# Level order in the recurrent heads, an exponential ahead of tile copies, and the output weights loaded during the merge

## The chip, the cores and the metric

The kernel runs on one core of a Trainium2 chip. The metric is the device time of one execution in microseconds; lower is better. The engines are TensorE (PE in the rows), VectorE (DVE), ScalarE (ACT), GpSimd (POOL) and SyncE (SP), each with an instruction queue of its own that runs in order and waits on semaphores.

## What is computed

The reference is a float32 block in two halves for 512 tokens of width 1024, with 256 context tokens in front of them in every recurrence. Three parts matter here. Two of them are recurrences with a decay for every channel, of this form, forwards and backwards, whose sum is the output:

```python
def step(s, inp):                     # one chunk of one head
    qc, kc, vc, gc = inp
    gcum = jnp.cumsum(gc, axis=2)
    decay = jnp.exp(jnp.where(causal[:, :, None],
                    gcum[:, :, :, None, :] - gcum[:, :, None, :, :], -jnp.inf))
    att = jnp.einsum('bhtd,bhtsd,bhsd->bhts', qc, decay, kc)
    o = einsum(att, vc) + einsum(qc * jnp.exp(gcum), s)
    s = exp(glast) * s + einsum(kc * jnp.exp(glast - gcum), vc)
```

In the first half of the block this is gated linear attention (4 heads, keys of 64, log-decay `log_sigmoid(..)/16`). In the second half it is 8 heads with keys of 128 whose forget gate `f = lb + (1 - lb) * sigmoid(x W)` gives `log f` and the keys `1 - f`. The head's output is normalised, multiplied by `silu` of a gate and collected. The third part is the end of the first half: `merged = gates_a * (ya W_a) + gates_b * (yb W_b)` and `merged @ w_o`, added to `x`.

## The kernel before

The kernel is a row of stages. Each is a block of one queue per engine, and a barrier follows it. A dense float32 product is made of three float32r products of halves (`product3`): ScalarE rounds a weight tile (`high`), VectorE or GpSimd takes the rest (`low`), TensorE multiplies. Eight such steps over the width make a lot (384 or 512 columns) in one of two PSUM banks, from which ScalarE copies it (`evict`). The SyncE queue loads weight tiles into two buffers, one tile when the half of the tile two before is made.

**Levels.** A chunk is 128 tokens. Its decay matrix isn't formed: seven levels, of block sizes 1 to 64, each cover the pairs that the level's middle splits. For a level, GpSimd subtracts cumulative logs (`hg_dec`), ScalarE takes the exponential, VectorE multiplies keys and queries (`mixed`, tile `hg_mix`), TensorE makes the products (`products`), and VectorE keeps the part under the level's mask (`kept`, tile `hg_att`). Level 0 is the diagonal. There are two buffers of each.

**Gated heads** (`gated_heads`, 8 heads). A head has 14 units; the order in each queue is written by hand with the unit's number `at`. TensorE first makes one whole head of projections (64 steps, `fill(64)`), and in the units of head h it makes the 64 steps of head h + 1: two forget tiles (lots 0 to 3), query (lot 4), value (5, 6), gate (7). Levels stand in the odd units, 1 to 13. Value and key transposes and the state updates of the forward direction stand at the start, those of the backward direction from unit 8. After unit 14 come 2 steps, the head's output product (`o_done`), 8 steps, and the sum of squares. ScalarE's gate activations for the next head (`forget`) stand in unit 10 with a table load on each side, the logs (`logs`) in unit 12, between two more loads. VectorE's scans of the next head stand after unit 14, around the last `kept`.

```python
for at in range(1, 2 * LV + 1):
    if at % 2 == 1:
        i = level_of(h, (at + 1) // 2)
        act.wait_ge(diff_ready, i)
        act.activation(dec[:, (i - 1) % DEC], ..., ACT.Exp).then_inc(dec_ready, 1)
```

**Pair attention** (`gla_pairs`, two pairs of heads) has the same scheme with 72 steps a pair, 24 of them ahead. Its levels already stand in units 1 to 7, one a unit, and its exponential of level k stands in unit k, behind the tile copies of the units before it. At the start ScalarE waits for three constants and takes the decay gates (`near`, `logs`) before its first `high`; VectorE takes `scans` before its first `low`.

**Merge and output product.** `merge` has eight steps; each loads 1 MB of gate weights and 0.5 MB of branch weights. `output_product` loads `w_o` (eight pieces of 0.5 MB) in its own stage and waits for all of them before its first matmul.

## Time and profile before

| what | value |
|---|---|
| time, median of 3 runs (lowest, highest) | 4791.02 us (4790.4, 4795.41) |
| time of the profiled execution | 4792.93 us |
| its span, first to last instruction | 4791.1 us |
| busy: TensorE, its weight loads, VectorE, ScalarE, GpSimd | 83%, 68%, 53%, 33%, 18% |
| mean granted TensorE clock, as a share of full | 0.902 |
| 195 to 426 us (pair attention): TensorE busy, clock | 177.67 of 231 us, 0.81 |
| 785 to 1010 us (first merge, output product) | 197.50 of 225 us, 0.93 |
| 1275 to 1843 us (gated heads) | 454.35 of 568 us, 0.89 |
| two gate weight loads of the merge, starts | 889.30 and 907.45 us |
| ScalarE: table load; cast of a weight tile; tile copy of 384, 512 columns; log of 768; exponential of a level | 1.28; 1.05; 0.48, 0.58; 0.84; 1.06 us |
| VectorE: rest of a weight tile; a level's two mixes; one keep; last-column difference; states of one direction; gated row | 1.22; 1.3; 0.73; 0.96; 1.8; 0.74 us |
| the same two mixes while GpSimd takes a difference (1590.73 to 1593.2 us) | 2.5 us |
| TensorE: a level's products at full clock | 1.06 us |

How to read it: the busy share of TensorE counts pipelined matmuls, so a busy engine isn't at its peak; granted clock 1.00 is 2.4 GHz and 0.50 is 1.2 GHz. In rows of waits, an engine and line waited for another engine's line: us in total, times, longest. In rows of the timeline: start, length, engine, line, operation, written and read tiles, count, and in square brackets the idle time before it and who ended it. Times are microseconds from the start of the span.

### The profile page before, as it was taken

What the parts mean: (1) busy time and instruction counts of PE and PEld (TensorE: products, weight loads), DVE (VectorE), ACT (ScalarE), POOL (GpSimd) and SP (SyncE); (2) the same over time, 40 slices, a digit from 0 to 9 for tenths busy, and PEclk for the clock granted to TensorE, in tenths of its full rate; (3) what the DMA queues carried; (4) which work ended last, traced back from release to release, by engine and by line L of the source; (5) the groups of instructions that cost most, each with busy time, mean ns of one, the idle gap of its engine ahead of it and who ended that gap; (6) DMA issues with size and microseconds to landing.
All of it is one profiled execution on the core that took longest, in us unless ns stands there. A gap on an engine that the chain in (4) does not pass through costs nothing. (4 is left out here: it accounts for less than half of the span.)

```text
span 4791.1 us, 52357 instructions
## 1 busy us (share of the span) xinstructions
PE 3962.1 (83%) x19735; PEld 3261.4 (68%) x19735; DVE 2516.8 (53%) x4208; ACT 1578.8 (33%) x2341; POOL 884.8 (18%) x445
## 2 busy tenths in 40 slices
PE   6387997869488885788886995698979999999995
PEld 5376986538377775677774552586767878888884
DVE  0354773110466663677774003699975555455555
ACT  0333332110344442455554002333653223223322
POOL 0021001100033321111111110242214422222221
PEclk9697999976689897999998997799999999999998
DMA  3011101223111101111112211232656533333331
GB/s 139 31 31 40 32 19 51 91 101 136 36 40 40 37 30 33 40 45 44 41 45 88 88 44 44 94 118 88 200 194 212 189 128 115 117 122 127 116 116 66
DMA packets 134894, 403.46 MB, mean 84 GB/s; under 512 B 16304, under 2 KB 55072, under 8 KB 125088
## 3 DMA queue, kind: packets, MB, share of 16 engines
q1 hardware_dynamic: 134688, 400.68, 24.7%
q8 instruction: 133, 2.18, 0.2%
q14 instruction: 73, 0.60, 0.0%
HBM read 348.18 MB, written 52.45 MB: 84 GB/s over the span
## 5 line engine op out<-in xcount | busy, mean ns | idle before, releaser
L2486 POOL TENSOR_TENSOR ex_vl<-ex_v,ex_vh 128x1024 fp32r<-128x1024 f32 x80 | 192.0, 2400 | 683.2 <-ACT ex_vh L2474 683.2
L243 PE MATMUL ps<-ex_xh,ex_ul 128*128 128x512 f32 x640 | 249.8, 390 | 8.1 <-DVE ex_ul L2493 8.1
L243 PE MATMUL ps<-hT_high,ma_wl 128*128 128x384 f32 (+1 forms) x576 | 233.0, 404 | 25.7 <-DVE ma_wl L3405 25.7
L244 PE MATMUL ps<-ex_xl,ex_uh 128*128 128x512 f32 x640 | 249.4, 390 | 0.0
L245 PE MATMUL ps<-ex_xh,ex_uh 128*128 128x512 f32 x640 | 249.4, 390 | 0.0
L2470 ACT ACTIVATE ex_ab<-ps 128x512 f32<-128x512 f32 x80 | 47.8, 598 | 610.4 <-PE ps L245 610.4
L243 PE MATMUL ps<-ex_vh,ex_al 128*128 128x512 f32 x640 | 249.0, 389 | 0.0
L244 PE MATMUL ps<-ex_vl,ex_ah 128*128 128x512 f32 x640 | 249.0, 389 | 0.0
L245 PE MATMUL ps<-ex_vh,ex_ah 128*128 128x512 f32 x640 | 249.0, 389 | 0.0
L2512 DVE TENSOR_TENSOR ex_acc<-ex_acc,ps 128x512 f32<-128x512 f32 x160 | 109.8, 688 | 248.0 <-PE ps L245 248.0
L1721 DVE TENSOR_TENSOR mg_sg<-mg_sg,ps 128x512 f32<-128x512 f32 x32 | 22.0, 687 | 405.2 <-PE ps L1691 404.6
L2507 DVE TENSOR_TENSOR ex_al<-ex_af,ex_ah 128x512 fp32r<-128x512 f32 x80 | 198.0, 2475 | 61.0 <-ACT ex_ah L2476 61.0
L150 PE MATMUL ps<-cond,mod_w 128*128 128x2 f32 x768 | 164.1, 352 | 70.3 <-DMA mod_w<-in_w_ada_cols 43.5
L2649 POOL TENSOR_TENSOR hg_dec<-hg_cum 128x512 f32<-128x512 f32 x56 | 82.2, 1469 | 730.4 <-DVE hg_cum L2913 577.6
L243 PE MATMUL ps<-hT_high,hg_wl 128*128 128x384 f32 (+1 forms) x512 | 194.2, 379 | 22.1 <-DVE hg_wl L2889 22.1
L150 PEld LDWEIGHTS ps<-cond,mod_w 128*128 128x128 f32 x768 | 164.0, 333 | 71.0 <-issue 71.0
L3101 POOL TENSOR_TENSOR ma_ce<-ma_ce,ma_c 128x512 f32<-128x512 f32 x64 | 94.5, 1477 | 637.2 <-ACT ma_ce L3304 637.2
L245 PE MATMUL ps<-hT_high,ma_wh 128*128 128x384 f32 (+1 forms) x576 | 206.7, 359 | 0.0
L244 PE MATMUL ps<-hT_low,ma_wh 128*128 128x384 f32 (+1 forms) x576 | 206.5, 359 | 0.0
L244 PE MATMUL ps<-hT_low,hg_wh 128*128 128x384 f32 (+1 forms) x512 | 186.8, 365 | 0.0
L245 PE MATMUL ps<-hT_high,hg_wh 128*128 128x384 f32 (+1 forms) x512 | 185.9, 363 | 0.0
L2218 DVE TENSOR_SCALAR sg_two<-iota,chosenT 128x128 f32<-128x128 f32 x512 | 183.9, 418 | 0.0
(509 smaller groups left out, 10735.0 us busy)
## 6 DMA issues: line engine op xcount, KB each, us to landing
ex_u<-in_peer_u SPq DMA_DIRECT2D x80, 512.0 KB, 4.3
ex_v<-in_peer_v SPq DMA_DIRECT2D x80, 512.0 KB, 4.2
gates_by_expert<-sg_gbuf SPq DMA_DIRECT2D x8, 4096.0 KB, 14.8
ma_w<-in_w_in_ma SPq DMA_DIRECT2D x48, 512.0 KB, 3.6
ev_v<-in_peer_v SPq DMA_DIRECT2D x48, 512.0 KB, 3.6
hg_w<-in_w_in_hg SPq DMA_DIRECT2D x40, 512.0 KB, 3.6
ex_g<-gates_by_expert SPq DMA_DIRECT2D x20, 1024.0 KB, 4.8
mg_wg<-in_w_merge SPq DMA_DIRECT2D x16, 1024.0 KB, 5.0
```

What stands on the lines that cost most here:

```text
L150: mm = pe.matmul(ps[:, n % 2, 2 * a:2 * a + 2], wt[:, a, k, :], conds[:, k, :], start=(k == 0), stop=(k == KD - 1))
L243: pe.matmul(out, a[1], b[0], start=start, stop=False)
L244: pe.matmul(out, a[0], b[1], start=False, stop=False)
L245: return pe.matmul(out, a[0], b[0], start=False, stop=stop)
L1721: link(dve.tensor_tensor(sg[:, n % 2, a, :], sg[:, n % 2, a, :], ps[:, b + 2 + a, :], ALU.mult))
L2218: ins = dve.tensor_scalar(two[:, t0 + a, :], iota, chosenT[:, 1, t:t + 1], chosenT[:, 2, t:t + 1], ALU.is_equal, ALU.mult)
L2470: act.activation(ab[:, j % 2, :], ps[:, j % 2, :], ACT.Gelu).then_inc(h_read, 1)
L2486: pool.tensor_tensor(vl[:, j], v[:, j % 2], vh[:, j].bitcast(F32), ALU.subtract).then_inc(vl_ready, 1)
L2507: dve.tensor_tensor(al[:, j], af[:, j % 2], ah[:, j].bitcast(F32), ALU.subtract).then_inc(al_ready, 1)
L2512: dve.tensor_tensor(acc[:, n // 2, n % 2, :], acc[:, n // 2, n % 2, :], ps[:, 2 + n % VB, :], ALU.add).then_inc(v_read, 1)
L2649: pool.tensor_tensor(ke, crossed(cums[:, h % 2], size, False, True), crossed(cums[:, h % 2], size, False, False), ALU.subtract)
L3101: pool.tensor_tensor(ce[:, i % 2], ce[:, i % 2], cT[:, P * c:P * c + P].unsqueeze(1).to_broadcast([P, J, P]), ALU.mult).then_inc(ce_scaled, 1)
```

## The change

Five edits, all in order or place; none changes what is computed.

1. `gated_heads`: levels stand in units 1 to 7, one a unit; ScalarE takes the exponentials of levels 1 and 2 in unit 1 and of level k + 1 in unit k, in front of that unit's tile copies. Transposes, updates, states, output product (now unit 10), gate activations (unit 8 and 9), logs (unit 10, behind the copy of lot 5), scans (unit 11), weighting and weight halves get new units. The sum of squares of head h stands in unit 2 of head h + 1. The query's activation is taken out of `forget` into `asked`; one table load a head goes. The 64 steps are spread by `FILL`.
2. `gla_pairs`: ScalarE's exponentials likewise one unit ahead.
3. `gla_pairs`: the first two `high` and `low` stand in front of the constants, gates and scans.
4. `merge` may load another tensor's rows during its steps 2 to 7; the first merge loads `w_o`.
5. `output_product` takes loaded weights and then neither loads nor waits.

```diff
         act.preload_act_table_set("natural_log_exp_and_others")
+        high(0)
+        high(1)
         act.wait_ge(const_in, 48)
         near(0, 0, 0)
         near(0, 1, 2)
         logs(0)
-        high(0)
-        high(1)
...
         for h in range(H):
             last, n = h + 1 == H, 6 * h
             for at in range(1, 2 * LV + 1):
-                if at <= LV:
-                    i = level_of(h, at)
+                for lv in (1, 2) if at == 1 else (at + 1,) if at < LV else ():
+                    i = level_of(h, lv)
...
+        low(0)
+        low(1)
+        dve.wait_ge(const_in, 48)
         near(0, 0, 0)
         near(0, 1, 2)
         dve.wait_ge(mask_in, 32)
-        dve.wait_ge(const_in, 48)
         scans(0)
-        for n in range(3):
-            low(n)
+        low(2)
         weighted(0, 0)
...
                 sp.dma_start(bT[:, 2 * g:2 * g + 2, :], b_dram[g]).then_inc(b_in, 16)
+            if n >= 2 and after is not None:
+                for j in range(n - 2, KD if n == KD - 1 else n - 1):
+                    sp.dma_start(after[0][:, j, :], after[1][P * j:P * j + P, :]).then_inc(after_in, 16)
+        if after is not None:
+            sp.wait_ge(after_in, 16 * KD)
 
     @block.gpsimd
     def _(pool):
...
+    loads = w is None
+    w = ctx.enter_context(core.sbuf("op_w", [P, KD, D], F32)) if loads else w
     y = ctx.enter_context(core.sbuf("op_y", [P, 2, 512], F32))
     with core.stage("w_in", "pe_done", "out_done", "dsteps") as (block, w_in, pe_done, out_done, dsteps):
         @block.sync
         def _(sp):
-            for j in range(KD):
-                sp.dma_start(w[:, j, :], w_dram[P * j:P * j + P, :]).then_inc(w_in, 16)
-            sp.wait_ge(w_in, 16 * KD)
+            if loads:
+                for j in range(KD):
+                    sp.dma_start(w[:, j, :], w_dram[P * j:P * j + P, :]).then_inc(w_in, 16)
+                sp.wait_ge(w_in, 16 * KD)
 
         @block.tensor
         def _(pe):
-            pe.wait_ge(w_in, 16 * KD)
+            if loads:
+                pe.wait_ge(w_in, 16 * KD)
             for n in range(8):
                 t, h = n // 2, n % 2
                 for j in range(KD):
...
-    tap("mT1", mT[:])
-    output_product(core, k, mT, d["w_o"], rows, 1.0, [xs[:, t, :] for t in range(NXC)])
+    with core.sbuf("op_w", [P, KD, D]) as w_o:
+        merge(core, k, hT, d["w_merge"], 4, 4, yaT, ybT, b_gate[:], mT, after=(w_o, d["w_o"]))
+        tap("mT1", mT[:])
+        output_product(core, k, mT, d["w_o"], rows, 1.0, [xs[:, t, :] for t in range(NXC)], w_o)
     with core.sbuf("final_g", [P, D], F32) as final_g:
...
-    LOW_AT = (1, 3, 6, 10, 13)
+    FILL = (4, 5, 5, 5, 5, 5, 5, 5, 5, 4, 5, 4, 4, 3)
...
+        def squares(h):
+            pe.wait_ge(sq_ready, h + 1)
+            pe.wait_ge(pre_ready, h + 1)
+            pe.matmul(ps[:, 5, :], k.ones[:], scr[:], start=True, stop=True).then_inc(ss_done, 1)
...
         products(0)
         for at in range(1, 2 * LV + 1):
...
+            if at <= LV:
+                products(at)
+            if at == 1:
+                pe.wait_ge(evicted, lot_of(h, V, 1) + 1)
                 for c in range(NC):
...
+                    mm = pe.transpose(turn(c), v[:, P * c:P * c + P], k.ident[:])
...
-            if at % 2 == 1:
-                products((at + 1) // 2)
-            fill(5 if at <= 8 else 4 if at <= 10 else 2 if at % 2 else 1)
...
-        fill(2)
-        pe.wait_ge(att_kept, (h + 1) * (LV + 1))
-        pe.wait_ge(S_ready, 2 * h + 2)
...
-        mm.then_inc(o_done, 1)
-        fill(8)
...
+            if at == 2:
+                key_rows(0)
+            if at == 3:
+                updates(0)
+            if at == 5:
+                key_rows(1)
+            if at == 6:
+                updates(1)
+            if at == 10:
+                pe.wait_ge(att_kept, (h + 1) * (LV + 1))
+                pe.wait_ge(S_ready, 2 * h + 2)
+                for c in range(NXC):
...
+                mm.then_inc(o_done, 1)
+            if at == 2 and h > 0:
+                squares(h - 1)
+            fill(FILL[at - 1])
+    squares(H - 1)
...
+    def asked(h):
         act.wait_ge(evicted, lot_of(h, Q) + 1)
...
     forget(0)
+    asked(0)
     evict(5)
     evict(6)
     high(5)
     logs(0)
     decays(0, 0)
+    decays(0, 1)
     for h in range(H):
         m, n, last = 8 * (h + 1), 5 * (h + 1), h + 1 == H
         for at in range(1, 2 * LV + 1):
-            dr = 0 if at <= LV else 1
-            u = 2 * h + dr
-            if at % 2 == 1:
-                i = level_of(h, (at + 1) // 2)
+            for lv in (1, 2) if at == 1 else (at + 1,) if at < LV else ():
+                i = level_of(h, lv)
                 act.wait_ge(diff_ready, i)
                 act.activation(dec[:, (i - 1) % DEC], dec[:, (i - 1) % DEC], ACT.Exp).then_inc(dec_ready, 1)
             if at == 1:
                 if h > 0:
-                    squares(h - 1)
+                    act.wait_ge(pre_ready, h)
+                evict(lot_of(h, G))
...
+                high(n + FB)
+            if at == 2 and not last:
+                evict(m)
+            if at == 3 and h > 0:
+                rstd(h - 1)
+            if at in (2, 5):
+                u = 2 * h + (0 if at == 2 else 1)
...
-            if at == 5:
-                decays(h, 1)
-            if at == 10:
+            if at == 4 and not last:
+                evict(m + 1)
+                high(n + Q)
+            if at == 5 and not last:
+                evict(m + 2)
+            if at == 7 and not last:
+                evict(m + 3)
+                high(n + V)
+            if at == 8:
                 act.preload_act_table_set("sigmoid_and_others")
                 if not last:
                     forget(h + 1)
+            if at == 9:
+                if not last:
+                    evict(m + 4)
+                    asked(h + 1)
+                    high(n + G)
                 act.wait_ge(evicted, lot_of(h, G) + 1)
                 opened(h)
-                act.preload_act_table_set("natural_log_exp_and_others")
-            if not last and at == 12:
-                logs(h + 1)
-        if not last:
-            evict(m + 5)
-            decays(h + 1, 0)
-            evict(m + 6)
-            high(n + 5 + FF)
-    squares(H - 1)
+            if at == 10:
+                if last:
+                    act.preload_act_table_set("natural_log_exp_and_others")
+                else:
+                    evict(m + 5)
+                    logs(h + 1)
+            if at == 11:
+                squares(h)
+            if at == 12 and not last:
+                decays(h + 1, 0)
+                decays(h + 1, 1)
+                evict(m + 6)
+            if at == 14 and not last:
+                high(n + 5 + FF)
...
     scan(0, 1)
+    low(5)
+    weighted(0, 0)
     for h in range(H):
-        weighted(h, 0)
+        n, last = 5 * (h + 1), h + 1 == H
         for at in range(1, 2 * LV + 1):
-            if at % 2 == 1:
-                mixed(h, (at + 1) // 2)
-            if at in LOW_AT:
-                low(5 * h + 5 + LOW_AT.index(at))
-            if at == 1 and h > 0:
-                pre(h - 1)
-            if at % 2 == 1:
-                kept(h, (at - 1) // 2)
-            if at == 3 and h > 0:
-                tail(h - 1)
+            if at <= LV:
+                mixed(h, at)
+            if at == 2:
+                low(n + FB)
+            if at <= LV + 1:
+                kept(h, at - 1)
+            if at == 3:
+                weighted(h, 1)
             if at == 4:
                 states(h, 0)
-            if at == 6:
-                weighted(h, 1)
-            if at == 11:
+            if at == 5:
+                low(n + Q)
+            if at == 8:
+                low(n + V)
                 states(h, 1)
-            if at == 12 and h + 1 < H:
+            if at == 9 and not last:
                 affine(h + 1, 0)
                 affine(h + 1, 1)
-                query(h + 1)
+            if at == 10:
+                if not last:
+                    query(h + 1)
+                opened(h)
+                low(n + G)
+            if at == 11 and not last:
+                scan(h + 1, 0)
+                scan(h + 1, 1)
             if at == 12:
-                opened(h)
-        if h + 1 < H:
-            scan(h + 1, 0)
-        kept(h, LV)
-        if h + 1 < H:
-            scan(h + 1, 1)
-    pre(H - 1)
+                pre(h)
+            if at == 13 and not last:
+                weighted(h + 1, 0)
+            if at == 14:
+                low(n + 5 + FF)
+            if at == 5 and h > 0:
+                tail(h - 1)
     tail(H - 1)
```

## Rows read from the trace of the kernel before

**Rows 1.** TensorE's waits in the gated heads, 1275 to 1843 us.

```profile
PE ps L2702 <- DVE hg_mix L2934: 82.8, 20, 7.8
...
PE ps L2742 <- DVE oT L2966: 12.7, 8, 2.2
```

**Rows 2.** Windows: busy of each engine with counts, then clock, DMA share, GB/s.

```profile
1512.68:1579.35 66.67, 56.02 (x321) 52.30 (x321) 42.02 (x57) 32.22 (x45) 20.76 (x14) 0.91 0.13 40
1579.00:1585.00 6.00, 5.66 (x27) 5.68 (x28) 5.96 (x7) 1.82 (x4) 0.00 (x0) 0.68 0.30 90
1595.00:1600.00 5.00, 4.84 (x23) 4.34 (x24) 0.70 (x2) 1.03 (x3) 1.47 (x2) 0.66 0.34 108
1637.00:1640.00 3.00, 2.93 (x13) 2.96 (x14) 2.82 (x8) 0.00 (x0) 0.00 (x0) 0.58 0.00 0
```

**Rows 3.** TensorE's timeline, products of a mixed level in the gated heads.

```profile
1329.85 2.08 PE L2702 MATMUL ps<-hg_mix 128*128 128x128 f32 x8 [0.15 <-DVE hg_mix L2934]
...
1568.87 1.75 PE L2702 MATMUL ps<-hg_mix 128*128 128x128 f32 x8 [3.13 <-DVE hg_mix L2934]
...
1579.35 2.04 PE L2702 MATMUL ps<-hg_mix 128*128 128x128 f32 x8 [6.19 <-DVE hg_mix L2934]
...
1800.31 0.94 PE L2702 MATMUL ps<-hg_mix 128*128 128x128 f32 x7
```

**Rows 4.** TensorE's timeline, first products of successive projection steps at full clock.

```profile
1743.43 0.34 PE L243 MATMUL ps<-hT_high,hg_wl 128*128 128x384 f32 x1
...
1743.96 0.34 PE L243 MATMUL ps<-hT_high,hg_wl 128*128 128x384 f32 x1
...
1791.77 0.40 PE L243 MATMUL ps<-hT_high,hg_wl 128*128 128x512 f32 x1
...
1792.47 0.40 PE L243 MATMUL ps<-hT_high,hg_wl 128*128 128x512 f32 x1
```

**Rows 5.** ScalarE's timeline around its gate activations.

```profile
1633.25 1.28 ACT L2871 ACT_TABLE_LOAD   x1
1634.54 1.06 ACT L2829 ACTIVATE hg_dec<-hg_dec 128x1024 f32<-128x1024 f32 x1
```

**Rows 6.** Timeline of the seam between heads 3 and 4.

```profile
1584.14 1.75 DVE L2913 TENSOR_TENSOR_SCAN hg_cum<-hg_restart,hg_f 128x768 f32<-128x768 f32 x1
...
1585.97 1.86 POOL L2649 TENSOR_TENSOR hg_dec<-hg_cum 128x512 f32<-128x512 f32 x1 [25.81 <-DVE hg_cum L2913]
...
1586.81 1.85 DVE L2923 TENSOR_TENSOR hg_kd<-hg_kd,hg_k 128x768 f32<-128x768 f32 x1
...
1588.58 1.58 DVE L2925 TENSOR_TENSOR hg_qe<-hg_qe,hg_q 128x512 f32<-128x512 f32 x1
...
1589.64 1.06 ACT L2829 ACTIVATE hg_dec<-hg_dec 128x1024 f32<-128x1024 f32 x1 [3.46 <-POOL hg_dec L2650]
```

**Rows 7.** TensorE's timeline, level 7 of the last head.

```profile
1828.47 0.76 PE L2702 MATMUL ps<-hg_mix 128*128 128x128 f32 x2 [2.90 <-DVE hg_mix L2934]
```

**Rows 8.** Timeline of pair attention: weight load, first step, one exponential.

```profile
199.02 0.90 SPq L489 DMA_DIRECT2D gla_w<-in_w_in_gla  x2
...
219.86 0.69 PE L243 MATMUL ps<-hT_high,gla_wl 128*128 128x384 f32 x1 [14.08 <-DVE gla_wl L785]
...
252.92 1.06 ACT L715 ACTIVATE ybT<-ybT 128x1024 f32<-128x1024 f32 x1
```

**Rows 9.** The page's DMA issues: KB each, us to landing.

```profile
hg_w<-in_w_in_hg SPq DMA_DIRECT2D x40, 512.0 KB, 3.6
...
mg_wg<-in_w_merge SPq DMA_DIRECT2D x16, 1024.0 KB, 5.0
```

**Rows 10.** TensorE's waits, 195 to 430 us.

```profile
PE ps L561 <- DVE gla_att L843: 14.0, 8, 3.4
```

**Rows 11.** Timeline around the first output product.

```profile
947.39 3.76 SPq L1736 DMA_DIRECT2D op_w<-in_w_o  x8
...
959.96 2.07 PE L1745 MATMUL ps<-op_w,mT 128*128 128x512 f32 x2 [15.93 <-DMA op_w<-in_w_o]
```

More of the change, by code:

```diff
@@ L1635, in _, with merge @@
                 tail(H - 1)
-def merge(core, k, hT, w_dram, nA, nB, aT, bT, gate_bias, mT, b_dram=None):
+def merge(core, k, hT, w_dram, nA, nB, aT, bT, gate_bias, mT, b_dram=None, after=None):
     nc = core.nc
@@ L1651, in merge @@
         sg = ctx.enter_context(core.sbuf("mg_sg", [P, 2, 2, NX], F32))
-        with core.stage("w_in*2", "g_in", "b_in", "high_ready", "low_ready", "gates_done", "pe_done", "sg_ready", "dsteps", "out_done") as (
-                block, w_in, g_in, b_in, high_ready, low_ready, gates_done, pe_done, sg_ready, dsteps, out_done):
+        with core.stage("w_in*2", "g_in", "b_in", "high_ready", "low_ready", "gates_done", "pe_done", "sg_ready", "dsteps", "out_done",
+                        "after_in") as (
+                block, w_in, g_in, b_in, high_ready, low_ready, gates_done, pe_done, sg_ready, dsteps, out_done, after_in):
             @block.sync
@@ L1722, in _, with output_product @@
                     dve.tensor_tensor(mT[:, n, :], sg[:, n % 2, 0, :], sg[:, n % 2, 1, :], ALU.add).then_inc(out_done, 1)
-def output_product(core, k, mT, w_dram, gate_row, alpha, xs):
+def output_product(core, k, mT, w_dram, gate_row, alpha, xs, w=None):
     nc = core.nc
@@ L2683, in _ @@
                     p = h % 2
-                    pe.wait_ge(evicted, lot_of(h, V, 1) + 1)
-                    for c in range(NC):
-                        mm = pe.transpose(turn(c), v[:, P * c:P * c + P], k.ident[:])
-                        if c in (3, NC - 1):
-                            mm.then_inc(vt_done, 1)
                     def products(lv):
@@ L2703, in products, with key_rows @@
                         mm.then_inc(att_done, 1)
+                    def squares(h):
+                        pe.wait_ge(sq_ready, h + 1)
+                        pe.wait_ge(pre_ready, h + 1)
+                        pe.matmul(ps[:, 5, :], k.ones[:], scr[:], start=True, stop=True).then_inc(ss_done, 1)
+                    def key_rows(dr):
+                        pe.wait_ge(kd_ready, 2 * h + dr + 1)
+                        if dr == 0:
+                            pe.wait_ge(vt_copied, 2 * h + 2)
+                        else:
+                            pe.wait_ge(S_ready, 2 * h + 1)
+                        for c in range(NC):
+                            mm = pe.transpose(turn(c), kds[:, dr, P * c:P * c + P], k.ident[:])
+                            if c in (3, NC - 1):
+                                mm.then_inc(kt_done, 1)
@@ L2705, in _, with updates @@
+                    def updates(dr):
+                        u = 2 * h + dr
+                        pe.wait_ge(kt_copied, 2 * u + 2)
+                        if u > 0:
+                            pe.wait_ge(S_ready, u)
+                        for c in ORDER[dr][:-1]:
+                            mm = pe.matmul(U(c), ktok[:, c, :], vt[:, c, :], start=True, stop=True)
+                        mm.then_inc(u_done, 1)
                     products(0)
                     for at in range(1, 2 * LV + 1):
-                        dr = 0 if at <= LV else 1
@@ L2722, in _ @@
-                        if at in (2, LV + 2):
-                            pe.wait_ge(kt_copied, 2 * u + 2)
-                            if u > 0:
-                                pe.wait_ge(S_ready, u)
-                            for c in ORDER[dr][:-1]:
-                                mm = pe.matmul(U(c), ktok[:, c, :], vt[:, c, :], start=True, stop=True)
-                            mm.then_inc(u_done, 1)
-                    fill(2)
-                    pe.wait_ge(att_kept, (h + 1) * (LV + 1))
@@ L2731, in _ @@
-                    pe.wait_ge(S_ready, 2 * h + 2)
-                    for c in range(NXC):
-                        o = ps[:, 5, P * c:P * c + P]
-                        pe.matmul(o, vt[:, C0 + c, :], att[:, c, :], start=True, stop=False)
-                        for dr in range(2):
-                            slot = ORDER[dr][C0:].index(C0 + c)
-                            mm = pe.matmul(o, S[:, dr, slot, :], qe[:, p, dr, P * c:P * c + P], start=False, stop=(dr == 1))
-                    mm.then_inc(o_done, 1)
@@ L2739, in _ @@
-                    fill(8)
-                    pe.wait_ge(sq_ready, h + 1)
-                    pe.wait_ge(pre_ready, h + 1)
-                    pe.matmul(ps[:, 5, :], k.ones[:], scr[:], start=True, stop=True).then_inc(ss_done, 1)
+                                    mm.then_inc(vt_done, 1)
+                        if at == 2:
[4 more added lines that the diff above has]
+                            key_rows(1)
@@ new lines, in _ @@
+                        if at == 6:
[4 more added lines that the diff above has]
+                            for c in range(NXC):
+                                o = ps[:, 5, P * c:P * c + P]
+                                pe.matmul(o, vt[:, C0 + c, :], att[:, c, :], start=True, stop=False)
+                                for dr in range(2):
+                                    slot = ORDER[dr][C0:].index(C0 + c)
+                                    mm = pe.matmul(o, S[:, dr, slot, :], qe[:, p, dr, P * c:P * c + P], start=False, stop=(dr == 1))
+                            mm.then_inc(o_done, 1)
```

35 lines of the change are left out of this document (1 added, 34 removed).

## The prediction

> **What bounds the kernel now.** The page first: TensorE is busy 83% of the span, no other engine over 53%; but its row in slices dips in the touched stages, and the row of the granted clock with it. The stages follow each other with a barrier between, so only time at the critical engine inside the three touched stages counts: pair attention (195 to 426 us), first merge and output product (785 to 1010), gated heads (1275 to 1843). The chain that ended last covers only the last 30 us of the span and says nothing on them. So I read, in this order, TensorE's waits per stage, the timeline around each wait, and the granted clock after it.
>
> In the gated heads TensorE waits 82.8 us for a mixed level, 20 times, and 12.7 us for the gated row (oT) in front of the sum of squares [rows 1]; its first weight tile isn't touched. The pattern repeats: from one late level to the same one in the next head it is 66.67 us, in which TensorE is busy 56.02; the idle 10.6 are waits of 3.13, 6.19 and, left over, some 1.3 [rows 2, 3]. From head 0 to head 7 the mean is (1800.31 - 1329.85)/7 = 67.2 us [rows 3]. After each pause the clock is granted at half (1.2 of 2.4 GHz) for a while: mean 0.68 in the 6 us after the 6.19, 0.66 in 5 us after the row wait, 0.58 in 3 us after the 3.13 [rows 2]. That loses 6 x 0.32 + 5 x 0.34 + 3 x 0.42 = 1.9 + 1.7 + 1.3 = 4.9 us. A head without pauses is 66.7 - 10.6 - 4.9 = **51.1 us**. Cross-check: a projection step of three products takes 0.53 us on 384 columns and 0.70 on 512 [rows 4]; 48 and 16 of them give 36.6 and leave 14.5 for attention.
>
> Why late: ScalarE runs in order and takes a level every second unit. In units 9 to 12 it first does two table loads of 1.28 and four sigmoids, then the exponential, and another load; meanwhile the level waits [rows 5]. GpSimd stands idle 46 of 67 us [rows 2].
>
> **The change, part by part.**
>
> *Gated heads, inside a head.* The seven levels move to units 1 to 7, an exponential one unit ahead and in front of the tile copies. Need against supply: a unit of TensorE is 1.06 for the level's products plus 4 or 5 steps, so 3.5 to 4.8 us with transposes and updates. A level costs GpSimd 20.76/7 = 3.0 us on average and 3.7 beside VectorE [rows 2, 6], ScalarE 1.06, VectorE 1.3 alone or 2.5 beside GpSimd plus 0.73 to keep it. All are under a unit, with two buffers. I walked the three queues through units 1 to 8 with these durations (the table ahead has the single ones): each level is ready 1 to 3 us before TensorE asks, tile copies and weight halves come before their steps, second states at +48 us from the first level for an output product at +53. So the 3.13, the 6.19 and the row wait go (squares now stand two units behind, in the next head). One table load of four a head goes too, in ScalarE's shadow.
>
> *Gated heads, at the seam.* The next head's logs now stand behind the copy of its value tile, which needs projection step 48 (end of unit 10). Call that t = 0. Copy 0.5; load 1.28, two logs to 3.4; first scan 2.7 to 4.5, difference to 5.4, second scan to 7.2; GpSimd's first level 3.7 to 10.9; exponential 11.9. VectorE meanwhile: difference 8.1, gated product 8.9, weighting 1.85 + 1.58 beside GpSimd to 12.2, weight half 1.22 to 13.4, mixed level 1.3 to 2.5, so ready at 14.7 to 15.9 [rows 6]. TensorE: 8 steps of 0.53 and 8 of 0.70 and the diagonal product, 10.9. It waits 3.8 to 5.0; I take **4.3**, plus 1.9 at half clock as after the 6.19. Queued behind the late level: value transposes, 4 steps, level 2; on VectorE the diagonal's copy. Period 51.1 + 4.3 + 1.9 = 57.3, and I add 0.5 for small waits: 57.8. Seven heads: 7 x (67.2 - 57.8) = 66 us.
> The Trainium skill, ScalarE: Activation LUTs, "What ACT_TABLE_LOAD costs", adds about 1.38 us of drain to each switch of set. The rows show none: a load starts at 1633.25, lasts 1.28, and the exponential starts at 1634.54 [rows 5]. By the page the wait would be about 1.4 longer in each of seven heads, 10 us less gain; the row decides.
>
> *Ends of that stage.* At the first head the sixth weight half now stands ahead of the weighting: level 1 about 1.4 us later; bounds 0 to 3. In the last head there are no steps to hide behind; 28.2 us pass from level 1 to level 7 [rows 3, 7]. VectorE's own queue for that stretch is six mixes (7.8 alone, 15 contended), keeps 5.1, weighting 1.6 to 3.4, states 1.8, tail 1: 17 to 26, I take 22; but the second states (1.8) no longer hide. Gain 4, bounds 0 to 9. The stage: 66 - 1.4 + 4 = **69 us**.
>
> *Pair attention, start.* The weight casts waited for the constants, three activations and two logs; the first projection step starts at 219.86 after 14.08 us of waiting, though its weights were asked for at 199.02 [rows 8]. Now cast and low half come first: landing at about 202.6 by the 3.6 us of such loads [rows 9], cast 1.0, half 1.2, ready before TensorE ends the gate-rate products at 205.8. Logs move 0.8 us later. The 24 steps end at about 222, the diagonal at 223.9; the first level then limits: last tile copy 222.8, cast 1.05, two exponentials, mix at about 227 against 241.5. Gain **14**, bounds 11 and 16.
>
> *Pair attention, levels.* The exponential stood behind a tile copy: it starts at 252.92, right behind a copy that waits for TensorE's lot [rows 8]; the mix and two keeps follow, and TensorE waits 1.4, 3.4, 0.5 and 1.6 us a head: 14.0 in all [rows 10]. One unit ahead they are covered by a unit of 4.9 us on TensorE against 3.9 to 4.3 on VectorE. The 3.4 also costs some 1.3 a head at half clock, as after the 3.13 above. Up to 16.6; the waits at the heads' starts stay, since level 1 is where it was. I take **15**, bounds 7 and 17.
>
> *Output weights.* The loads now start when the product's stage opens, 947.39, and TensorE starts at 959.96 [rows 11]. In the merge there are 18 us between 1 MB pieces that land in 5.0 [rows 9], so 0.5 MB more a step is covered; the last pieces land by about 920. The order costs nothing there: SyncE's queue holds only these loads, and an extra 3 x 0.4 us of issue at the end blocks nobody. TensorE can start where SyncE did, at about 947.9: **12**, bounds 11 and 14 (a shorter half-rate start). The second merge is as before.
>
> *Sum.* 69 + 14 + 15 + 12 = 110 us. The profiled execution took 4792.93 (span 4791.1), 1.9 above the median of 4791.02: 4793 - 110 = 4683, as a median **4681**.
>
> **The rivals.**
> A, forecast: the seam keeps 2 to 7 us: 4660 to 4706. 0.61.
> B, the seam is hidden: logs come earlier than my walk, all pauses go. 7 x (67.2 - 51.5) = 110, stage 113, time 4637. For it: GpSimd and VectorE have room on average (21 and 42 us of 67 [rows 2]). Against: the step-48 copy fixes the logs. 0.09.
> C, the seam keeps 8 to 12 us: contention of GpSimd with VectorE's two-input operations (the 1.85 and 3.7 us [rows 6] are of such an overlap) or one more wait in the chain. Period 61 to 66, stage 26, time about 4724. 0.18. The Trainium skill, GPSIMD Engine Reference, in its table of the engine says its SBUF interfaces are shared with VectorE when that has two SBUF inputs. That speaks against packing the levels, and would make C of a full overlap; the sum above holds that overlap at the seam already.
> D, the gated heads' change does nothing: the pauses move whole to the seam (a late level there costs what two cost before). Only the other 41 us stay: 4750. 0.08.
> E, slower: ScalarE waits for step 48, TensorE's steps 45 to 48 wait behind the output product, which waits for states(1) behind VectorE's value half, behind ScalarE's cast. If that ring closes late, every head stalls at units 10 and 1. It takes 41/7 = 5.9 us a head above 67.2, that is a seam of 20 us instead of 4.3, to cross. By the walk states come 5 us early. At 25 us: about 4820. 0.03. The last 0.01 is within 0.2%.
>
> **How the numbers follow.** Predicted 4681. The range takes A, the near side of B and most of C: 4648 to 4730 (A alone 4660 to 4706). A change of 0.2%, about 10 us, is what a measurement can tell; faster 0.95, same 0.02, slower 0.03.
>
> **What the next profile would show.** TensorE's waits on mixed levels in the gated heads fall from 20 to about 7 to 9, one a head at level 1, sum 30 us plus the last head; no wait on the row of the norm; period 57 to 58 us. Pair attention's first projection step at about 206; waits on kept levels near zero but for level 1. Output product at about 12 us behind the last merge step. The prediction is wrong if waits appear at projection steps (a tile copy or half too late), at value transposes, or at level 2 or 3 because VectorE carries the low half and the weighting in front of them.

## The result, and the profile after

The changed kernel takes **4674.86 us** (median of 4 runs, 4669.97 to 4675.12) against 4792.42 us for the kernel before (4 runs, 4790.4 to 4795.41) on the same chip: 0.9752 of it, interval 0.9735 to 0.9769, or 117.6 us less. The forecast was 110 less. The span is 4673.3 us.

The stages run one behind the other, so the time between the first weight loads of successive stages shows where it went (worked out from the starts of the loads of `gla_w`, `gdn_w`, `mg_wg`, `hg_w`, `proj_w` and the first matmul on `op_w`):

| stretch | before | after | difference | forecast |
|---|---|---|---|---|
| pair attention (`gla_w` to `gdn_w`) | 227.8 | 189.1 | -38.7 | -29 (14 + 15) |
| first merge to its output product (`mg_wg` to `op_w`) | 175.0 | 162.6 | -12.4 | -12 |
| gated heads (`hg_w` to `proj_w`) | 573.2 | 503.4 | -69.8 | -69 |
| all the rest | 3815.1 | 3818.2 | +3.1 | 0 |

The rest is in stages that the change leaves alone. In the thirteen traces of this document, one of each kernel and a second of the changed one, this rest takes 3813.0 to 3820.3 us, so its 3.1 are what differs from trace to trace. Where a run leaves pair attention as it is after the change, the stage repeats within 188.8 to 190.1 us, the merge to its product within 162.1 to 162.6, and the gated heads within 503.4 to 505.6.

**Gated heads.** The changed kernel's TensorE waits from 1210 to 1730 us (engine and line, for whom, us in total, times, longest), which answer to [rows 1] (mixed levels, the stage's first weight tile, the second states, the gated row):

```profile
PE ps L2708 <- DVE hg_mix L2963: 49.6, 13, 10.1
PE ps L243 <- DVE hg_wl L2918: 22.5, 1, 22.5
PE ps L2759 <- DVE hg_S L2984: 2.6, 1, 2.6
PE ps L2714 <- DVE oT L2995: 1.6, 1, 1.6
```

The waits on a mixed level fell from 82.8 to 49.6 us and those in front of the sum of squares from 12.7 to 1.6, once instead of 8 times. Where the 13 stand is in TensorE's timeline, the answer to [rows 3]. The rows are level 1 of heads 0, 2 and 7 (those of heads 1 and 3 to 6 wait 5.05 to 5.07 us), and last, level 7 of head 7:

```profile
1281.63 2.07 PE L2708 MATMUL ps<-hg_mix 128*128 128x128 f32 x8 [10.14 <-DVE hg_mix L2963]
...
1397.46 2.01 PE L2708 MATMUL ps<-hg_mix 128*128 128x128 f32 x8 [5.07 <-DVE hg_mix L2963]
...
1686.94 1.42 PE L2708 MATMUL ps<-hg_mix 128*128 128x128 f32 x8 [3.90 <-DVE hg_mix L2963]
...
1708.10 1.13 PE L2708 MATMUL ps<-hg_mix 128*128 128x128 f32 x8 [0.30 <-DVE hg_mix L2963]
```

One wait a head is left, always at level 1: 10.14 us in the first head, 5.05 or 5.07 in the next six, 3.90 in the last. From the second head on this is the wait at the seam, where a new head's levels follow the units of the head before. Levels 2 to 7 wait for nothing until the last head, where five of them wait 5.2 us together. The period, from level 1 of one head to level 1 of the next, is (1686.94 - 1281.63)/7 = 57.9 us, against 67.2 before. The windows of one head and of the 5 us behind its wait (us, busy of PE, PEld, DVE, ACT, POOL, clock, DMA share, GB/s), beside [rows 2]:

```profile
1397.46:1455.73 58.27, 53.20 (x321) 50.29 (x321) 44.64 (x57) 30.86 (x45) 19.04 (x15) 0.97 0.15 46
1397.46:1402.46 5.00, 5.00 (x24) 5.00 (x25) 3.46 (x4) 2.23 (x5) 4.37 (x4) 0.66 0.12 47
```

The same 321 matmuls keep TensorE busy 53.20 instead of 56.02 us, because the mean clock over a head rose from 0.91 to 0.97. The clock is still granted at half behind the wait that is left (0.66 in 5 us), which loses 5 x 0.34 = 1.7 us.

What the wait is made of shows in the timeline of the seam before head 2 in the changed kernel:

```profile
1381.79 0.48 ACT L2784 COPY hg_v<-ps 128x384 f32<-128x384 f32 x1 [4.13 <-PE ps L245]
...
1382.29 1.28 ACT L2804 ACT_TABLE_LOAD   x1
...
1383.58 1.58 ACT L2807 ACTIVATE hg_f<-hg_f 128x768 f32<-128x768 f32 x2
...
1387.13 1.75 DVE L2942 TENSOR_TENSOR_SCAN hg_cum<-hg_restart,hg_f 128x768 f32<-128x768 f32 x1
...
1388.96 1.88 POOL L2660 TENSOR_TENSOR hg_dec<-hg_cum 128x512 f32<-128x512 f32 x1 [30.48 <-DVE hg_cum L2942]
...
1390.45 1.20 DVE L2952 TENSOR_TENSOR hg_kd<-hg_kd,hg_k 128x768 f32<-128x768 f32 x1
...
1391.58 1.57 DVE L2954 TENSOR_TENSOR hg_qe<-hg_qe,hg_q 128x512 f32<-128x512 f32 x1
1392.56 1.49 POOL L2660 TENSOR_TENSOR hg_dec<-hg_cum 128x512 f32<-128x512 f32 x1
1392.63 1.06 ACT L2856 ACTIVATE hg_dec<-hg_dec 128x1024 f32<-128x1024 f32 x1 [0.57 <-POOL hg_dec L2661]
1393.07 2.06 DVE L2918 TENSOR_TENSOR hg_wl<-hg_w,hg_wh 128x1024 fp32r<-128x1024 f32 x1
...
1395.05 1.66 DVE L2962 TENSOR_TENSOR hg_mix<-hg_dec,hg_k 128x512 f32<-128x512 f32 x1
...
1396.63 0.68 DVE L2963 TENSOR_TENSOR hg_mix<-hg_dec,hg_q 128x512 f32<-128x512 f32 x1
```

ScalarE idles 4.13 us for projection step 48, copies its tile, and only then loads the table and takes the logs. From that copy to the mixed level it is 1397.46 - 1381.79 = 15.7 us; TensorE has other work for 10.6 of them. GpSimd had been idle 30.48 us when its first level could start.

**Pair attention.** TensorE's timeline in the changed kernel, first projection step and level 1 of both pairs:

```profile
205.64 0.69 PE L243 MATMUL ps<-hT_high,gla_wl 128*128 128x384 f32 x1
...
227.07 3.09 PE L561 MATMUL ps<-gla_mix 64*128 64x128 f32 x16 [2.90 <-DVE gla_att L838]
...
310.67 3.09 PE L561 MATMUL ps<-gla_mix 64*128 64x128 f32 x16 [4.38 <-DVE gla_att L838]
```

The first step waits for nothing (14.08 before, [rows 8]). Its waits list has no entry for kept levels under the mask any more (14.0 before, [rows 10]); the two for the diagonal, 7.3 together, stay. From level 1 to level 7 of pair one and of pair two, windows of the kernel before (same columns as above):

```profile
241.50:285.60 44.10, 37.01 (x217) 33.67 (x217) 20.61 (x28) 10.32 (x15) 10.76 (x10) 0.88 0.06 21
334.59:380.51 45.92, 38.88 (x216) 35.61 (x217) 20.62 (x28) 10.31 (x15) 10.17 (x10) 0.83 0.00 1
```

and of the changed kernel:

```profile
227.07:261.70 34.63, 34.63 (x216) 31.75 (x216) 22.64 (x29) 10.43 (x15) 10.80 (x10) 0.91 0.08 27
310.67:344.62 33.95, 33.95 (x217) 31.08 (x217) 22.60 (x29) 10.43 (x15) 10.75 (x10) 0.93 0.00 1
```

The two level stretches are 9.5 and 12.0 us shorter. TensorE's idle time gives 7.1 and 7.0 of that; the other 2.4 and 4.9 are the same matmuls, done in less time at a higher clock. Behind the second pair's level 7 the stage ends 43.5 us later (388.1 - 344.6) instead of 46.3 (426.8 - 380.5); there too it is the clock, 0.71 instead of 0.66, with TensorE busy 31.95 instead of 34.76 us.

**Output product.** Its first matmul in the changed kernel, beside [rows 11]:

```profile
908.90 4.08 PE L1755 MATMUL ps<-op_w,mT 128*128 128x512 f32 x5 [3.47 <-PEq L69]
```

It waits 3.47 us for the stage's barrier where it waited 15.93 for its weights.

### The profile page after: what moved, and what is told of

Its sections match the earlier page's. It is cut to its first block and busy times, and to the rows that moved or that the text cites. A ratio compares the mean times of both kernels' runs of the same rounds, so it can differ in the third digit from the quotient of the medians.

```text
span 4673.3 us, 52352 instructions
## 1 busy us (share of the span) xinstructions
PE 3933.1 (84%) x19735; PEld 3238.1 (69%) x19735; DVE 2539.2 (54%) x4208; ACT 1570.4 (34%) x2334; POOL 872.3 (19%) x445
## 5 line engine op out<-in xcount | busy, mean ns | idle before, releaser
L2660 POOL TENSOR_TENSOR hg_dec<-hg_cum 128x512 f32<-128x512 f32 x56 | 69.9, 1248 | 664.5 <-DVE hg_cum L2942 599.1
```

The costliest lines, as they stand in the source:

```text
L2660: pool.tensor_tensor(ke, crossed(cums[:, h % 2], size, False, True), crossed(cums[:, h % 2], size, False, False), ALU.subtract)
```

## Experiments

All start from the changed kernel; diffs are against it. Each time was measured together with runs of the kernel before (4793.4 us for the first four, 4793.04 for the next four, 4792.52 for the last three), and ratios with their intervals are to that. An interval of 0.0016 on either side is about 8 us, wider than most differences here. So the readings go by stage lengths, taken from one trace of each kernel as in the table above.

### The gated heads as before

The whole function is put back, all else stays.

```diff
 def gated_heads(...):
-    FILL = (4, 5, 5, 5, 5, 5, 5, 5, 5, 4, 5, 4, 4, 3)
+    LOW_AT = (1, 3, 6, 10, 13)
...
+                        if at % 2 == 1:
+                            products((at + 1) // 2)
+                        fill(5 if at <= 8 else 4 if at <= 10 else 2 if at % 2 else 1)
```

> The changed kernel with the gated heads of the kernel before. Theory: the gated heads' part is worth 69 us alone (stage starts 118.9 us earlier after it against 50.2 before it), nothing of it comes from other stages: about 4744, and the stage's rows as before (20 waits on mixed levels, 82.8 us). Rival: the parts help each other (clock carried over from one stage to the next), then the cost of undoing differs from 69 by more than 5 us.

4739.27 us, 0.989 (0.9873 to 0.9906). The stage takes 571.8 us, 68.4 more than in the changed kernel. TensorE's waits in it are back:

```profile
PE ps L2713 <- DVE hg_mix L2945: 80.1, 20, 7.8
...
PE ps L2753 <- DVE oT L2977: 11.2, 8, 2.1
```

The whole run costs 64.4 us more, 4 less than the stage: the stages that no edit touches took 3814.0 us in this trace and 3818.2 in the changed kernel's, which is within their spread. So 68 to 70 us belong to this function; help from other stages of a few us is not excluded by whole runs, but no stage length shows any.

### Pair attention's exponentials back in their own units

```diff
-                        for lv in (1, 2) if at == 1 else (at + 1,) if at < LV else ():
-                            i = level_of(h, lv)
+                        if at <= LV:
+                            i = level_of(h, at)
```

> The changed kernel with pair attention's exponentials back in their own units behind the tile copies; its early casts stay. Theory: this edit alone is worth 24 us, 14 of pauses and 10 of half clock that followed them: about 4699. Rival one: the half clock costs only 1.3 us a head as forecast, and the rest of the 38.7 us of that stage belongs to the early casts: about 4691. Rival two: the pauses are absorbed later in the stage: under 4 us.

4695.09 us, 0.9796 (0.978 to 0.9813). The stage takes 213.2 us, 24.1 more. Its TensorE waits from 195 to 415 us:

```profile
PE ps L561 <- DVE gla_att L843: 14.1, 9, 3.4
```

14.1 us of pauses cost 24.1 us. The other 10 are TensorE's own work at a lower clock: levels 1 to 7 of the first pair (226.46 to 270.59 us of this kernel) take 44.13 us and keep it busy 36.98 at a clock of 0.89, for the 216 matmuls that take 34.63 in the changed kernel; the kernel before has 37.01. The time of the run, 4695.09, lies midway between the 4699 of the theory and the 4691 of rival one and can't tell them apart; the stage's 24.1 us can, since the early casts stayed and rival one allows it 17.

### Only the last three exponentials back

Levels 1 to 4 stay ahead, 5 to 7 stand in their own unit, behind its tile copies.

```diff
-                        for lv in (1, 2) if at == 1 else (at + 1,) if at < LV else ():
+                        for lv in {1: (1, 2), 2: (3,), 3: (4,)}.get(at, (at,) if 5 <= at <= LV else ()):
```

> Exponentials of levels 2 to 4 ahead, those of levels 5 to 7 back in their own units. Only the two smaller pauses of a pair (0.5 and 1.6 us) come back, 4.4 us in all. Theory: a pause this short is not followed by much half clock, so 4 to 6 us above the changed kernel (4679 to 4681) and the 3.4 us pause is what brings the half clock. Rival: half clock follows every pause in proportion: 24 x 4.4/14 = 7.5 us, about 4682 or more.

4680.81 us, 0.9767 (0.9751 to 0.9783). The stage takes 198.3 us, 9.2 more. Three pauses a pair came back, not two. TensorE's waits in it:

```profile
PE ps L561 <- DVE gla_att L843: 5.4, 6, 1.6
```

and the pauses of the first pair in its timeline:

```profile
250.17 1.76 PE L561 MATMUL ps<-gla_mix 64*128 64x128 f32 x16 [0.53 <-DVE gla_att L843]
...
256.39 1.76 PE L561 MATMUL ps<-gla_mix 64*128 64x128 f32 x16 [0.48 <-DVE gla_att L843]
...
263.82 1.76 PE L561 MATMUL ps<-gla_mix 64*128 64x128 f32 x16 [1.65 <-DVE gla_att L843]
```

None of the six is above 1.65 us, yet the stage pays 3.8 us beyond their 5.4, give or take the 1.3 by which the stage differs between traces. The clock in the 5 us behind the last pause of the first pair, and of the second:

```profile
263.82:268.82 5.00, 5.00 (x34) 4.38 (x35) 2.92 (x4) 0.86 (x2) 0.00 (x0) 1.00 0.30 105
350.20:355.20 5.00, 5.00 (x28) 4.39 (x29) 2.92 (x4) 0.86 (x2) 0.00 (x0) 0.71 0.02 5
```

It is 1.00 behind the two smaller pauses of the first pair as well. Between level 1 and level 7 the pairs pay 0.5 and 0.7 us beyond their pauses, at the changed kernel's clock (0.91 and 0.93 in both); the other 2.5 come behind the second pair's level 7 (46.0 us to the end of the stage against 43.5), whose 1.65 us pause is the one with half clock behind it (5 x 0.29 = 1.5 us of them; the last 1 us isn't explained). So the theory holds for five of the six pauses and fails for one. The time of the run fits the theory's 4679 to 4681, the stage's length the rival's 7.5 us or more: the rival has the size, but half clock doesn't follow every pause.

### Constants, gates and scans ahead of the first weight casts

```diff
-                high(0)
-                high(1)
                 act.wait_ge(const_in, 48)
...
                 logs(0)
+                high(0)
+                high(1)
```

VectorE's first two `low` go behind the scans likewise.

> The changed kernel with pair attention's first two casts and halves back behind the constants, gates and scans. Theory: 14.4 us (first level's products at 227.1 us against 241.5), about 4689. Rival: the stage's later levels were waiting for more than this start, then 20 us or more.

4686.06 us, 0.9781 (0.9764 to 0.9797); the stage takes 14.5 us more. TensorE's first step in this kernel:

```profile
220.83 0.69 PE L243 MATMUL ps<-hT_high,gla_wl 128*128 128x384 f32 x1 [14.07 <-DVE gla_wl L785]
```

### The next head's logs ahead of the step-48 copy

```diff
                             else:
-                                evict(m + 5)
                                 logs(h + 1)
+                                evict(m + 5)
```

> In the gated heads' unit 10 ScalarE takes the next head's logs before the value tile's copy that waits for projection step 48. Theory: the wait of 5.07 us at each head's first level hangs on that copy; logs 4 us earlier shorten it to about 1, 28 us off in seven heads and up to 1.9 us of half clock each on top: 4634 to 4647. Rival: VectorE's queue in front of the first mixed level (weighting 2.8, weight half 2.1) sets the wait: under 5 us gained, about 4672.

4635.14 us, 0.9669 (0.9653 to 0.9686): 0.992 of the changed kernel, by the two ratios to the kernel before (0.9669 and, in the run of the changed kernel below, 0.9747). The stage takes 465.1 us, 38.3 less. Level 1 of heads 2 and 3:

```profile
1384.16 1.13 PE L2708 MATMUL ps<-hg_mix 128*128 128x128 f32 x8 [0.91 <-DVE hg_mix L2963]
...
1436.64 1.13 PE L2708 MATMUL ps<-hg_mix 128*128 128x128 f32 x8 [0.92 <-DVE hg_mix L2963]
```

The seam's wait falls from 5.07 to 0.9 and the period to 52.5 us. The chain behind the logs is as long as it was; only its start came off step 48. So it was the order of one copy and the logs in ScalarE's queue that set the seam. The wait that is left has no half clock behind it. Head 2, and the 5 us behind its wait:

```profile
1384.16:1436.64 52.48, 51.56 (x321) 48.64 (x321) 45.44 (x57) 30.77 (x45) 20.05 (x15) 1.00 0.16 51
1384.16:1389.16 5.00, 5.00 (x38) 5.00 (x39) 4.77 (x4) 2.90 (x5) 4.37 (x4) 1.00 0.14 52
```

The same 321 matmuls at full clock keep TensorE busy 51.56 us. The floor that the prediction worked out from one head was 51.1, 0.5 too low.

### The mixed level ahead of weighting and weight half

VectorE takes level 1's mixes before the next weight half, the diagonal's copy and the weighting.

```diff
+                        if at == 1 and h > 0:
+                            low(n + FF)
+                            kept(h, 0)
+                            weighted(h, 0)
...
-                        if at == 13 and not last:
-                            weighted(h + 1, 0)
-                        if at == 14:
-                            low(n + 5 + FF)
```

> VectorE takes the next head's first mixed level in front of the weight half and the weighting. Theory (logs set the wait): the exponential is ready 1.4 us before VectorE comes to it, so 1.4 us a head, about 10 us in all: 4665; part may come back as a wait for turned keys in unit 2. Rival (VectorE's queue sets it): 3 us or more a head, 4650 or less.

4665.47 us, 0.973 (0.9713 to 0.9746); the stage takes 8.7 us less. Levels 1 and 2 of head 2:

```profile
1394.29 2.05 PE L2708 MATMUL ps<-hg_mix 128*128 128x128 f32 x8 [2.91 <-DVE hg_mix L2963]
...
1400.02 1.13 PE L2708 MATMUL ps<-hg_mix 128*128 128x128 f32 x8 [0.26 <-DVE hg_mix L2963]
```

2.16 us of the wait were VectorE's queue, more than the theory's 1.4 and less than the rival's 3; the work put off comes back as 0.26 to 1.87 us at level 2 in five heads. The half clock stays: behind the 2.9 us it is 0.67 over 5 us in this head. VectorE idles 2.52 us for the exponential in front of the mixes here, so the rest of the wait, 2.9, is not its own.

### Both

> Both orders together. Theory: the wait at the seam goes altogether, with its half clock: 7 x (5.07 + 1.9) = 49 us, 4626, a head of 51.1 to 52 us. Rival: the weighting now late makes TensorE wait for turned keys in unit 2, and the head stays above 54 us: 4645 or more.

4634.3 us, 0.9667 (0.9651 to 0.9684); the stage takes 465.4 us, the same as with the logs alone, with a wait of 1.02 at each level 1 where that one has 0.91. The two gains don't add: with the chain early enough, VectorE's order no longer matters. The theory was wrong by 8 us, since the wait doesn't go altogether; the rival's 54 us a head isn't there either (52.6). What sets the last microsecond isn't shown.

### One more table load in front of the logs

```diff
                 def logs(h):
+                    act.preload_act_table_set("sigmoid_and_others")
                     act.preload_act_table_set("natural_log")
```

> One more activation table load in front of the logs of every head. Theory: the logs are on the chain that ends in the first level, so each load costs its 1.28 us: 7 x 1.28 = 9 us, 4684. The Trainium skill's page ScalarE: Activation LUTs adds about 1.38 us of drain to a switch, which would make 7 x 2.66 = 19 us, 4694. Rival (VectorE's queue sets the wait): nothing, 4675.

4688.53 us, 0.9778 (0.9761 to 0.9794); the stage takes 13.7 us more.

```profile
1402.81 2.04 PE L2708 MATMUL ps<-hg_mix 128*128 128x128 f32 x8 [6.34 <-DVE hg_mix L2964]
```

The seam's wait goes from 5.07 to 6.34: 1.27 us, the load's own 1.28 and nothing else. The waits on mixed levels sum to 60.4 instead of 49.6, in eight heads, since the first head's logs have the load too; the other 2.9 us of the 13.7 are TensorE's own work at a lower clock. Those 2.9 are badly measured: two traces of the changed kernel, with the same waits, differ by 2.2 us in this stage (503.4 and 505.6), in TensorE's busy time. The run's 4688.53 lies midway between 4684 and 4694; the wait's own row decides between them. This load has no activation between itself and the next load, so it doesn't test a drain behind an activation; the seam's rows do, below.

### The output weights loaded in their own stage

```diff
-            merge(core, k, hT, d["w_merge"], 4, 4, yaT, ybT, b_gate[:], mT, after=(w_o, d["w_o"]))
+            merge(core, k, hT, d["w_merge"], 4, 4, yaT, ybT, b_gate[:], mT)
```

> The changed kernel with the output weights loaded in the output product's own stage again. Theory: 12 us, the landing time alone (its first product came 12.4 us sooner behind the start of the merge's loads): about 4687. Rival: the extra loads slow the merge's steps, so undoing costs less than 11 us.

4686.51 us, 0.9779 (0.9763 to 0.9795). From the merge's first load to the product it is 175.2 us, 12.8 more than in the changed kernel measured beside it (162.4).

```profile
919.59 5.67 PE L1755 MATMUL ps<-op_w,mT 128*128 128x512 f32 x7 [16.03 <-DMA op_w<-in_w_o]
```

### The changed kernel once more

Run beside the one above and the one below.

> The changed kernel itself, beside the others of this call. Both theories: 4675 within 5 us; it tells how far times differ from chip to chip.

4673.09 us (4667.14 to 4676.0), 0.9747 (0.9731 to 0.9763).

### Logs first, and the second pair's first exponential earlier

Beside the logs' order, pair attention's second pair takes its first exponential and mixed level ahead of the norm's logarithm and exponential.

```diff
-                        for lv in (1, 2) if at == 1 else (at + 1,) if at < LV else ():
+                        for lv in ((1, 2) if h == 0 else (2,)) if at == 1 else (at + 1,) if at < LV else ():
...
                             high(n + 6 + V1)
+                            if not last:
+                                i = level_of(h + 1, 1)
+                                act.wait_ge(diff_ready, i)
+                                act.activation(dec[:, (i - 1) % DEC], ..., ACT.Exp, scale=RATE).then_inc(dec_ready, 1)
```

> The kernel with the logs first, and in pair attention the second pair's first exponential and mixed level in front of the normalisation's last steps. Theory: the 4.4 us wait at the second pair's first level hangs on the logarithm and exponential of the norm in ScalarE's queue, then 4 us and about 2 us of half clock go: 4629 against 4635 for the logs alone. Rival: the projection that fills the query tile ends last, then nothing: 4635.

4633.72 us (4631.28 to 4637.14), 0.9668 (0.9652 to 0.9684): the fastest median, but no different from the logs' order alone (4635.14, 0.9669), and not the 4629 of the theory. Pair attention takes 189.2 us, as without it. VectorE's timeline of this kernel in front of the second pair's level 1, and the product itself:

```profile
308.94 0.69 DVE L831 TENSOR_TENSOR gla_mix<-ybT,gla_k 128x512 f32<-128x512 f32 x1
309.54 0.69 DVE L832 TENSOR_TENSOR gla_mix<-ybT,gla_q 128x512 f32<-128x512 f32 x1
310.24 1.23 DVE L917 TENSOR_TENSOR yaT<-yaT,gla_scr 128x1024 f32<-128x1024 f32 x1
311.38 1.28 DVE L842 SCALAR_TENSOR_TENSOR gla_att<-ps,ident 128x512 f32<-128x512 f32 x2
...
312.12 3.10 PE L561 MATMUL ps<-gla_mix 64*128 64x128 f32 x16 [4.12 <-DVE gla_att L842]
```

The mixed level is ready at 310.2, but level 1's products wait for the diagonal's copy out of PSUM, and that stands behind the norm's product. The wait goes from 4.38 to 4.12. The list of waits had said so by its releaser, `gla_att`, not `gla_mix`: the edit moved the wrong instruction of VectorE's queue.

## Why the prediction was right

The forecast case, A, came in: the seam keeps 5.07 us. 4675 us lies in A's own 4660 to 4706 and 6 us under the predicted 4681. Point by point:

- **Waits inside a head** (the 3.13, the 6.19 and the row wait go): right. No level but the first waits in heads 0 to 6, and the row wait shows once, 1.6 us.
- **Seam**, forecast 3.8 to 5.0, taken 4.3: measured 5.07, just above the top. The walk had 14.7 to 15.9 us from step 48 to the mixed level; it is 15.7. Its order of VectorE's work was the right one, its weight half too short: 2.06 us beside GpSimd, where I had allowed 1.22; the two mixes took 2.3, within the 1.3 to 2.5. The experiment with the mixes first measures that queue at 2.16 us. Half clock 1.7, forecast 1.9.
- **Period**, forecast 57.8: measured 57.9. That the two agree so closely is luck: the seam was 0.8 too short and the floor 0.5 too low (51.6 with the logs first), and the 0.5 us added for small waits, which weren't there, and 0.2 too much of half clock made up for half of that. By the parts, 51.6 + 5.07 + 1.7 = 58.3, which is head 2 (58.27); the first and the last period are shorter (57.3 and 56.9). Seven heads are 7 x (67.2 - 57.9) = 65 us, forecast 66.
- **First head**, forecast 1.4 later: from the first projection step to level 1 it is 49.9 us, 1.6 more than before, within the bounds 0 to 3. Here a 10.14 us wait on the mixed level stands where 6.70 on the value's transposes and 0.15 stood; my list of waits left this one out, so its "30 us plus the last head" became 49.6 (34.3 at seven seams, 10.1, and 5.2 in the last head), and its 7 to 9 waits became 13, five of them in the last head.
- **Last head**, forecast 4 less (0 to 9): from level 1 to the stage's last norm row it is 34.1 us against 40.7, 6.6 less. Levels 1 to 7 take 21.2 us; the walk of VectorE's queue said 22.
- **Pair attention, start**, 14: 14.4 by the trace (241.50 - 227.07), 14.5 when undone.
- **Pair attention, levels**, 15: this is the term that was mis-sized. The pauses came out as forecast, 14.0 to nothing. But I priced the half clock at 1.3 us a head, for the longest pause alone. It is 10 us in all: 24.3 by the trace (9.5 + 12.0 + 2.8 behind level 7) and 24.1 when undone. The bounds, 7 and 17, left it out too. This one term, 9 us short, is more than the whole error of 7.6; the stages left alone took 3.1 back. The rows before held the number: TensorE was busy 37.01 and 38.88 us for the two level stretches, at clocks of 0.88 and 0.83, and not only behind the 3.4 us pauses.
- **Output weights**, 12: 12.4 by the trace, 12.8 when undone. My sign for it, the product "about 12 us behind the last merge step", was worded wrongly: it is 3.47 us behind the last merge matmul, 12.5 us sooner than before.

Undone one at a time, the parts cost 68.4 + 24.1 + 14.5 + 12.8 = 119.8 us in their stages, and the change as a whole saved 120.9 in them: by stage lengths they are independent, the two edits inside pair attention too (24.1 + 14.5 against 38.7). Whole runs say this less sharply: the four medians lie 64.4, 20.2, 11.2 and, against the changed kernel beside it, 13.4 us above, 109 in all, with about 8 us of interval on each.

**The rivals.** B (seam hidden, 4637) was no property of this change, but the run with the logs first is what it describes: 4635 us, stage 38 us shorter, period 52.5 where B had 51.5. The argument against B, that the step-48 copy fixes the logs, is now shown rather than argued. C needed a seam of 8 to 12 and D needed pauses that move whole: neither was there. For E, TensorE's waits in the changed kernel name neither a tile copy nor a second state in heads 0 to 6; only in the last head 2.6 us go to the states.

**The rules that were weighed.** A table load at 1382.29 lasts 1.28 and the logarithm starts at 1383.58, while one more load moves the seam by 1.27. The drain of some 1.38 us that the Trainium skill, ScalarE: Activation LUTs, "What ACT_TABLE_LOAD costs", adds to a switch isn't in either; the measurement decides. The overlap on which C rested does cost: by VectorE's timelines the mix of 128 x 512 takes 1.66 us beside GpSimd and 0.68 alone, the weight half 2.06 against 1.21. That agrees with the shared interfaces in the engine's table of the Trainium skill, GPSIMD Engine Reference. By these figures it costs an estimated 2 us a head at the seam (0.98 and 0.85), where VectorE is on the path, and nothing at levels 2 to 7 of heads 0 to 6, where TensorE waits for none of them.

## What to carry to other kernels

When an in-order queue feeds a long chain in the next iteration, look for a wait of that queue on late work (here a PSUM copy) in front of the chain's first instruction; swapping two lines there was worth 38 us, more than half of what the whole reordering of that function gave. Price many small pauses of a dense TensorE stretch by the clock granted over the whole stretch, which the profile before shows, not by the pauses and what follows the longest of them. And move what the list of waits names as releaser, after following that engine's queue back, not what computes the data one thinks of.

## What the runs showed that was not expected

- **The half clock behind short pauses.** In pair attention nine pauses of up to 3.4 us, 14.1 together, cost 24.1 us, and six of at most 1.65, 5.4 together, cost 9.2. Both are 1.7 times the pauses, but in the second case only one of the six has half clock behind it. In the gated heads the runs vary the length of one wait a head. Over the 5 us behind it, in heads 1 to 6, the clock is 1.00 each time behind 0.9 us (logs first) and behind 1.0 (both orders), 0.50 to 0.72 behind 2.9 in five heads and 1.00 in the sixth (mixed level first), 0.61 to 0.70 behind 5.07, and 0.50 to 0.71 behind 6.34. So a single price per us of pause doesn't fit these rows: the clock has to be read behind each wait. The 38 us of the logs first are the plainest case: 26.8 are waits, and the other 11.5 are clock.
- **Work in the shadow is free only while it stays there.** The weight half (2.06 us) and the weighting in front of the mix were on the path in the changed kernel, and moving them was worth 8.7 us; with the logs first it was worth nothing (4634.3 against 4635.14).
